# Four softmax attentions of a two-block transformer kernel, regrouped to 512 score columns a step, and differential weights combined ahead of normalising

## The reference, cut to what matters

```
global (8 query heads, 2 key heads, d = 64): softmax(q k^T / 8) v                       512 x 512 scores a head
dilated (3 groups of 4 heads): s = q k^T / 8 + bias, masked to |offset| <= reach
    lse = logsumexp(s); o = exp(s - lse) v
    out = sum over groups of softmax(lse)_group * o_group
differential (8 heads, two score maps m = 0, 1 each, causal):
    p_m = softmax(q_m k_m^T / 8 + rel_bias);  out = (p_0 - lambda p_1) v
window (8 heads, 2 key heads, a query block sees its own and the block before):
    s = q k^T / 8 + bias;  p = exp(s - max) / (sum exp(s - max) + exp(sink - max));  out = p v
```

## Time and profile before

| | |
|---|---|
| median of 3 executions | 3630.17 (3629.97 to 3633.74) |
| profiled execution, its own time | 3633.27 |
| its span | 3631.5 |
| mean granted PE clock over the span | 0.919 of full speed |
| busy: PE, PEld, DVE, ACT, POOL | 3201.4, 2543.0, 2324.2, 1214.5, 374.9 |
| first-layer attention stage, twice | 213.6 to 347.3 and 1097.5 to 1231.2 |
| differential attention stage | 1985.6 to 2087.4 |
| window attention stage | 3131.2 to 3201.2 |

### The profile page before, as it was taken

The page is one execution under the profiler, slowest core; times in us unless marked ns, Lnnn a source line. Parts: engine busy times, 40 slices in busy tenths (PEclk is TensorE's granted clock), DMA queues, the critical chain, the costliest instruction groups (busy, mean ns, idle before and its releaser), DMA issues. The chain is left out here.

```text
span 3631.5 us, 40689 instructions
## 1 busy us (share of the span) xinstructions
PE 3201.4 (88%) x14731; PEld 2543.0 (70%) x14731; DVE 2324.2 (64%) x3761; ACT 1214.5 (33%) x1713; POOL 374.9 (10%) x136
## 2 busy tenths in 40 slices
PE   4999996996799896899499789889999898989999
PEld 3777775774676685777377578757887687658887
DVE  6766666897676657599733747667664575564445
ACT  2323224664323322476322624431111222231111
POOL 0000001000000000100000000304444000004443
PEclk9999996998799998799789799989999899869999
DMA  7751724997655353599652034024442452103222
GB/s 256 238 171 61 242 101 141 360 405 278 216 171 168 135 185 99 193 401 403 243 170 100 1 102 139 27 82 133 148 144 74 136 182 79 53 24 105 92 92 81
DMA packets 285304, 583.89 MB, mean 161 GB/s; under 512 B 21561, under 2 KB 129537, under 8 KB 278076
## 3 DMA queue, kind: packets, MB, share of 16 engines
q1 hardware_dynamic: 272744, 537.83, 42.8%
q10 hardware_dynamic: 7764, 26.85, 1.8%
q0 software_dynamic: 4608, 16.78, 1.2%
HBM read 529.44 MB, written 78.70 MB: 167 GB/s over the span
## 5 line engine op out<-in xcount | busy, mean ns | idle before, releaser
L132 ACT CAST w_hi<-ring 128x2048 fp32r<-128x2048 f32 (+2 forms) x166 | 308.1, 1859 | 1213.5 <-PE ps L283 1030.9
L283 PE MATMUL ps<-hT_hi,w_hi 128*128 128x512 f32 (+1 forms) x1256 | 501.1, 399 | 25.2 <-DVEq L1117 12.6
L283 PE MATMUL ps<-hT_lo,w_hi 128*128 128x512 f32 (+1 forms) x1256 | 498.6, 397 | 0.0
L139 POOL TENSOR_TENSOR w_lo<-ring,w_hi 128x2048 fp32r<-128x2048 f32 x64 | 307.2, 4802 | 935.9 <-ACTq L2854 552.7
L144 DVE TENSOR_TENSOR w_lo<-ring,w_hi 128x2048 fp32r<-128x2048 f32 (+3 forms) x112 | 245.4, 2195 | 233.5 <-ACT w_hi L132 233.2
L283 PE MATMUL ps<-hT_hi,w_lo 128*128 128x512 f32 (+1 forms) x1256 | 305.2, 395 | 10.2 <-DVE w_lo L144 10.2
L283 PEld LDWEIGHTS ps<-hT_hi,w_hi 128*128 128x128 f32 (+1 forms) x1256 | 238.6, 190 | 85.6 <-DVEq L1117 14.2
L283 PEld LDWEIGHTS ps<-hT_hi,w_lo 128*128 128x128 f32 (+1 forms) x1256 | 235.7, 188 | 67.3 <-DVE w_lo L144 12.2
L1054 DVE SCALAR_TENSOR_TENSOR piece_sums<-pieces,cond,piece_sums 128x512 f32<-128x512 f32 x294 | 220.7, 751 | 90.4 <-DMA pieces<-in_w_ada_dram 57.8
L283 PEld LDWEIGHTS ps<-hT_lo,w_hi 128*128 128x128 f32 (+1 forms) x1256 | 238.6, 190 | 55.5
L283 PE MATMUL ps<-w_hi,hT_hi 128*128 128x512 f32 (+1 forms) x672 | 259.9, 389 | 1.0 <-ACT w_hi L132 1.0
(11 more groups left out here) (594 smaller groups left out, 6258.3 us busy)
## 6 DMA issues: line engine op xcount, KB each, us to landing
ring<-in_mlp_w_dram SPq DMA_DIRECT2D x64, 1024.0 KB, 5.2
pieces<-in_w_ada_dram SPq DMA_DIRECT2D x96, 512.0 KB, 6.0
ring<-in_w_in_dram SPq DMA_DIRECT2D x36, 1024.0 KB, 7.0
pieces<-in_mod_w_dram SPq DMA_DIRECT2D x72, 512.0 KB, 5.3
raw_sep<-in_w_exp_gate_dram SPq DMA_DIRECT2D x50, 512.0 KB
raw_sep<-in_w_exp_up_dram SPq DMA_DIRECT2D x50, 512.0 KB
raw_sep<-in_w_exp_down_dram SPq DMA_DIRECT2D x24, 1024.0 KB
ring<-in_e_w_in_dram SPq DMA_DIRECT2D x24, 1024.0 KB, 5.5
```

What stands on the lines that cost most here:

```text
L132: self.k.nc.scalar.copy(self.k.parts[0][:, i, 0:words], self.k.ring[:, i, 0:words]).then_inc(self.high, 1)
L139: self.k.nc.gpsimd.tensor_tensor(self.k.parts[1][:, i, 0:words], self.k.ring[:, i, 0:words], self.k.parts[0][:, i, 0:words].bitcast(F32), ...
L283: mm = pe.matmul(out, a if weight_left else b, b if weight_left else a, start=first and part == 0 and q == ks[0] and o == 0, stop=last and ...
```

## The change

- **Groups.** The units become groups of 512 score columns in one bank: one head of the global attention, four heads of 128 columns, or two heads of 256. First layer: 32 global groups and 16 dilated ones (for each tile two with four heads, two with two). Window: 2 groups of four heads (t = 0) and 12 of two. A group's heads have one parity.
- **Scores.** PE issues the scores of groups a and a+1 together, in every second step; a's heads read partitions 0 to 63, a+1's 64 to 127, and they take turns. The order of the global units changes to suit.
- **Maxima.** DVE takes the maximum of group i+1 in step i (before, of i). With a bias it is now an add and a reduce over all heads. For four dilated heads a third instruction adds the negated maxima by broadcast, and ACT's exponential is one instruction over 512 columns; otherwise one per head. The dilated sums are no longer accumulated: v has a column of ones, so that the product yields 65 columns a head. The signs of maxima and sink are turned, which saves the negation.
- **Copies of transposes** go to ACT for odd global groups and for all dilated and window groups. Scores' and exponentials' buffers become three each.
- **Window.** 28 instead of 12 warm-up matmuls.
- **Differential.** The maxima come out negated (scale -1, minimum) and aren't linked; map 1 is scaled by the ratio of the sums times -lambda and added to unscaled map 0, and ACT's output copy multiplies by map 0's reciprocal. The full-width scaling and the negation are gone.
- **Around it.** `U1` and `U2` become `U12`, heads are stored by parity, `v0`, `v0c`, `vc` get the column of ones, and `branches` merges with the new layout.

The diff, cut to its core:

```diff
 def attention(k, groups, loads=(), space=None, late=(), ahead=None, warm=12):
-        pr, sc, pT = idle[:, 0:4], idle[:, 4:6], idle[:, 6:8]
+        pr, sc, pT = idle[:, 0:3], idle[:, 3:6], idle[:, 6:8]
+        by_act = [u["kind"] != "global" or i % 2 == 1 for i, u in enumerate(groups)]
...
         def _(pe):
+            def scores(a):
+                b = a + 1
+                if b >= 4:
+                    pe.wait_ge(exp_done, b - 3)
+                for h in range(heads(a)):
+                    last_a, last_b = score(a, h), score(b, h)
+                last_a.then_inc(s_ready, 1)
+                last_b.then_inc(s_ready, 1)
+            warm_up(k, pe, 4, warm)
             for i in range(-2, N + 2):
-                if i + 2 < N:
-                    n, u = i + 2, units[i + 2]
-                    if n >= 4:
-                        pe.wait_ge(exp_done, n - 3)
-                    pe.matmul(k.ps[:, bank[n % 4], 0:W(n)], u["q"], u["k"], start=True, stop=True).then_inc(s_ready, 1)
+                if i % 2 == 0 and i + 2 < N:
+                    scores(i + 2)
...
         def _(act):
+            def soften(i):
+                u = groups[i]
+                act.wait_ge(max_done, i + 1)
+                if i >= 3:
+                    act.wait_ge(t_ready, i - 2)
+                if i >= 4 and u["kind"] != "dilated":
+                    act.wait_ge(o_out, i - 3)
+                p = pr[:, i % 3]
+                if u["kind"] == "global":
+                    last = nc.scalar.activation(p, k.ps[:, bank[i % 4], :], ACT.Exp, bias=nm(i), accum_out=ls[:, i % 4, 0:1])
+                elif u["kind"] == "dilated" and heads(i) == 4:
+                    last = nc.scalar.activation(p, sc[:, i % 3], ACT.Exp)
+                else:
+                    if u["kind"] == "window":
+                        nc.scalar.activation(es[:, i % 4, 0:heads(i)], es[:, i % 4, 0:heads(i)], ACT.Exp)
+                    for h in range(heads(i)):
+                        last = nc.scalar.activation(p[:, at], sc[:, i % 3, at], ACT.Exp, bias=nm(i)[:, h:h + 1], accum_out=total)
+                last.then_inc(exp_done, 1)
+            for i in range(N + 1):
+                if i < N:
+                    soften(i)
+                v = i - 1
+                if v >= 0 and by_act[v]:
+                    act.wait_ge(t_ready, v + 1)
+                    if v >= 2:
+                        act.wait_ge(o_ready, v - 1)
+                    nc.scalar.copy(pT[:, v % 2], k.ps[:, 2 + v % 2, :]).then_inc(t_act, 1)
...
         def _(dve):
+            def maxima(i):
...
+                x = per_head(sc[:, i % 3], i)
+                link(V.tensor_tensor(x, per_head(s, i), u["bias"], ALU.add))
+                ins = V.tensor_reduce(nm(i), x, AX, ALU.max, negate=True)
+                if u["kind"] == "window":
+                    link(ins)
+                    link(V.tensor_tensor(nm(i), nm(i), u["less_sink"], ALU.min))
+                    ins = V.tensor_tensor(es[:, i % 4, 0:heads(i)], nm(i), u["less_sink"], ALU.subtract)
+                elif heads(i) == 4:
+                    link(ins)
+                    ins = V.tensor_tensor(x, x, bcast(nm(i), 2, width(i)), ALU.add)
+                ins.then_inc(max_done, 1)
...
+            for i in range(-1, N + 2):
+                if i + 1 < N:
+                    maxima(i + 1)
+                v = i - 1
+                if 0 <= v < N and not by_act[v]:
...
+                    V.tensor_copy(pT[:, v % 2], k.ps[:, 2 + v % 2, :]).then_inc(t_dve, 1)
                 if i >= 2:
+                    result(i - 2)
...
 def diff_attention(...)
-                        pe.wait_ge(max_done, n - 1)
+                        pe.wait_ge(max_done, 2 * n - 2)
-                    nc.scalar.copy(y[:, t, h * P:(h + 1) * P], k.ps[:, 6 + u % 2, 0:P]).then_inc(o_out, 1)
+                    nc.scalar.activation(y[:, t, h * P:(h + 1) * P], k.ps[:, 6 + u % 2, 0:P], ACT.Copy, scale=inv[:, u % 4, 0:1]).then_inc(o_out, 1)
-                        link(V.tensor_tensor_reduce(sc[:, i % 2, m, 0:W(i)], k.ps[:, 2 * (i % 2) + m, 0:W(i)], b, 1.0, 2 * NEG,
-                                                    ALU.add, ALU.max, mx[:, i % 2, m:m + 1]))
-                    V.tensor_scalar(nm[:, i % 2, :], mx[:, i % 2, :], -1.0, None, ALU.mult).then_inc(max_done, 1)
+                        V.tensor_tensor_reduce(sc[:, i % 2, m, 0:W(i)], k.ps[:, 2 * (i % 2) + m, 0:W(i)], b, -1.0, -2 * NEG,
+                                               ALU.add, ALU.min, nm[:, i % 2, m:m + 1]).then_inc(max_done, 1)
...
-                    link(V.reciprocal(l, l))
-                    link(V.tensor_tensor(l[:, 1:2], l[:, 1:2], nlam[:], ALU.mult))
+                    link(V.reciprocal(inv[:, u % 4, :], l))
+                    link(V.scalar_tensor_tensor(r, l[:, 0:1], inv[:, u % 4, 1:2], nlam[:], ALU.mult, ALU.mult))
-                    link(V.tensor_scalar(p0, p0, l[:, 0:1], None, ALU.mult))
-                    V.scalar_tensor_tensor(p0, p1, l[:, 1:2], p0, ALU.mult, ALU.add).then_inc(p_ready, 1)
+                    V.scalar_tensor_tensor(p0, p1, r, p0, ALU.mult, ALU.add).then_inc(p_ready, 1)
```

More of the change, by code:

```diff
@@ L188, in constants @@
         for h in range(BG):
[L189 removed]
+            band[:, e, h % 2, h // 2] = np.where(ok, -slope[h] * dist.astype(f), f(NEG))
     out["bias_band"] = band
@@ L1561, in qkd_dst, with attention @@
     return dst, p, mul
-def attention(k, units, loads=(), space=None, late=(), ahead=None):
+def attention(k, groups, loads=(), space=None, late=(), ahead=None, warm=12):
     nc = k.nc
@@ L1647, in _ @@
             link = Link(dve, step)
[L1648 to L1664, removed]
-                        link(nc.vector.tensor_tensor_reduce(sc[:, i % 2, 0:W(i)], s, u["bias"], 1.0, 2 * NEG, ALU.add, ALU.max, m))
-                        if u.get("sink") is not None:
-                            link(nc.vector.tensor_tensor(m, m, u["sink"], ALU.max))
-                        nc.vector.tensor_scalar(n, m, -1.0, None, ALU.mult).then_inc(max_done, 1)
-                i = ahead - 1
-                if 1 <= i <= N:
-                    v = i - 1
@@ new lines, in result @@
+            def result(v):
+                u, n = groups[v], heads(v)
+                dve.wait_ge(o_ready, v + 1)
+                d = u["heads"][0][2][0].shape[-1]
+                po = k.ps[:, 4 + v % 2, 0:n * d]
+                if u["kind"] == "dilated":
+                    V.tensor_copy(u["out"], po.rearrange("p (h d) -> p h d", h=n)).then_inc(o_out, 1)
+                    return
+                l = ls[:, v % 4, 0:n]
+                if u["kind"] == "window":
+                    link(V.tensor_tensor(l, l, es[:, v % 4, 0:n], ALU.add))
+                link(V.reciprocal(l, l))
+                if n == 1:
+                    V.tensor_scalar(u["out"], po, l, None, ALU.mult).then_inc(o_out, 1)
+                else:
+                    V.tensor_tensor(u["out"], po.rearrange("p (h d) -> p h d", h=n), bcast(l, 2, d), ALU.mult).then_inc(o_out, 1)
@@ new lines, in global_groups, with dilated_groups @@
+    return groups
+def dilated_groups(T, band, cls):
+    groups = []
+    for t in range(NT):
+        for odd in range(2):
+            rows, heads = slice(64 * odd, 64 * odd + 64), []
+            for g in range(2):
+                for half in range(2):
+                    q, kk = (T[n][rows, 2 * g + half, t * P:(t + 1) * P] for n in ("qcT", "kcT"))
+                    heads.append((q, kk, [T["vc"][:, t, BG * g + 2 * half + odd, :]]))
+            u = T["U12"][:, 2 * t + odd].rearrange("p g h d -> p (g h) d")
+            groups.append(dict(kind="dilated", heads=heads, bias=cls[:, odd], out=u[:, :, 0:HD + 1], nm=u[:, :, HD + 1]))
+        for odd in range(2):
+            rows, heads = slice(64 * odd, 64 * odd + 64), []
+            for half in range(2):
+                heads.append((T["q0T"][rows, half, t * P:(t + 1) * P], T["k0T"][rows, half, t * P:t * P + 256],
+                              [T["v0"][:, t + j, 2 * half + odd, :] for j in range(2)]))
+            u = T["U0"][:, 2 * t + odd]
+            groups.append(dict(kind="dilated", heads=heads, bias=band[:, 0 if t == 0 else 2 if t == NT - 1 else 1, odd],
+                               out=u[:, :, 0:HD + 1], nm=u[:, :, HD + 1]))
+    return groups
@@ L3579, in odd_mixer @@
             ring = lambda i: k.ring[:, i, :].rearrange("p (k n) -> p k n", k=4)
-            attention(k, units, space=space, late=moves, ahead=[(ring(i), wo[:, KD:KD + 4, 512 * i:512 * (i + 1)]) for i in range(2)])
+            attention(k, groups, warm=28, space=space, late=moves, ahead=[(ring(i), wo[:, KD:KD + 4, 512 * i:512 * (i + 1)]) for i in range(2)])
             hT = pair_of(nc, h, "hT", [P, KD, S], side="right")
```

207 lines of the change are left out of this document (105 added, 102 removed).

## The result

The changed kernel takes 3523.57 us in the median (3518.82 to 3526.11, 4 runs) against 3630.42 (3629.97 to 3633.74, 4 runs): ratio 0.9702, 95% interval 0.9685 to 0.9719. The profiled execution has a span of 3524.3 us.

What follows compares the result with a forecast made beforehand. PE was taken to bound the global part, DVE and PE nearly tied in the dilated part, in-order PE and low clock mattering elsewhere. Gains of 62 (first layer), 8 (differential) and 7 (window) sum to 77 us: 3553 us, range 3526 to 3582.

Steps and rivals of the forecast that it cites:

- Some fours will stay up: I take 8: Differential stage: gain of 8 us (5 to 20), with the clock up for some sets of four units.
- I take low: 7: Window stage: clock lost in the idle start and low after, gain of 7 us (3 to 22).
- the clock stays up in both: Rival for the differential and window stages: gains of 16 and 21 us, 99 in all, kernel 3531 us; chance 0.20.
- once low, never regained it: Window stage: the old stage never regained the clock level though PE was busy throughout; basis for taking 7 us, not 21.
- a DVE wait for scores of over 1 us in each four: Differential stage: sign expected in the profile, with the stage at about 93 us.
- clock up throughout: Differential stage: four units take 8.9 us against 10.85, a gain of 15.6 us.
- the 2.5 of the rival: Rival for the dilated groups: DVE bounds them at 2.5 us each, gain 64 us, kernel 3566 us; chance 0.16.
- Early maxima and ACT's copies: Global part of the first layer: both moves worth nothing by themselves, hidden in PE's time.
- Loads: First dilated maximum: all loads must have landed, now needed earlier; over 4 us of cover, so cost nothing.
- pairs that don't overlap: Rival for the paired scores: no overlap, global period still 2.48 us, gain 44 us, kernel 3586 us; chance 0.07.
- a low clock in the first layer: Rival: PE falls to the low level there, 3.65 us a group, kernel 78 us slower at 3708; chance 0.04.
- no change: Rival for the whole kernel: time within 0.2% (7 us), gains offset by unseen waits such as late loads; chance 0.02.

Runs made afterwards that it cites:

- late_maxima: The changed kernel with each maximum taken in step i as before, not one group early: 3598.83 us, ratio 0.9892 to the kernel before.
- window_unpaired: The changed kernel with window groups for t > 0 ordered so that both groups of a pair have one parity: 3531.52 us, ratio 0.9727 to the kernel before.
- diff_filled: The kernel before with dummy matmuls where PE idles in the differential stage: 3620.56 us, ratio 0.9971 to the kernel before.
- fused: The changed kernel with each head's add and maximum fused into one DVE instruction: 3507.06 us, ratio 0.9650 to the kernel before.
- copies_dve: The changed kernel with the transposes' copies of all global groups on DVE, none on ACT: 3548.40 us, ratio 0.9744 to the kernel before.
- diff_alone: The kernel before with the change's differential edit and nothing else: 3615.98 us, ratio 0.9950 to the kernel before.

## Why the prediction was wrong

**The step that failed is the clock in the two short stages.** "Some fours will stay up: I take 8" and "I take low: 7" chose the lower end of each range from the behaviour of the old stages. The rival in which the clock stays up in both (62 + 16 + 21 = 99 us, chance 0.20) came nearest: the stages gave 101.9. That is partly luck, for the clock did not stay up in either (0.94 and 0.76).

- Window: the sizes were right (3.55 for 3.65, 2.31 for 2.45, warm-up 3.7 for 3.4), and so was the loss of the level in the idle start. (The forecast's terms for DVE sum to 2.30 to 2.59 and not to the 2.42 to 2.55 that stand there; it changes nothing.) Wrong was "once low, never regained it", read from one trace and carried over. The Trainium skill ("TensorE: Matmul & The Clock Gate", Part 1, What's actually happening) says that activity releases the throttle; the prediction set it aside because the old trace disagreed, and here the level came back behind 12 us of unbroken PE work. So from its first score the stage ran low for 22 of 44.7 us, where the sum had it low throughout. In late_maxima, where PE went on idling about a third or more of every second window of 4 us, it came back for 3.4 us only. Why the old stage did not regain it in 40 us with PE busy throughout stays open: the level can come back without pairing (window_unpaired), and the size of the groups was not tried alone.
- Differential: both terms were undersized. The prediction took 5.6 us for the edit with the clock mixed as before, since DVE's saving would turn into waiting for PE at the low level, and 2.4 more for the clock. The edit is worth 10.5 us at clock 1.00, and the clock the other 8.6 of the stage's 19.1, of the 10.0 that holding it brought the old stage. The forecast sign, a DVE wait for scores of over 1 us in each four, came (0.85 + 0.32 us); the stage's time did not. The prediction's "clock up throughout" (8.9 us for four units, 15.6 in all) was itself 0.3 us a four too high: they take 8.59. At clock 1.00 the old four takes 10.08 us (diff_filled, with its dummies), not 10.85.
- First layer: right within 3 us, partly by cancelling. The global part gave 32 x 0.595 = 19.0 a call for 16.8: overlap 13.6, and 5.4 from taking groups two by two, which was not in the sum. The dilated part took 2.05 for 2.1 and gave 16.5; the ends cost 2.1 for 1.4 in the first call. The second gave 31.9, for 3.4 us at its start ran at the low level. The tie of DVE and PE went to DVE, at 2.05, not at the 2.5 of the rival. The Trainium skill's warning that evacuation may become the bound ("TensorEngine Tiling (Array Packing)", Performance Considerations, PSUM Bottleneck) is borne out in part: in the dilated and window groups DVE, which adds the bias to the scores out of PSUM but also reduces them, was the bound, as fused shows (2.05 to 1.895 us a group); in the global ones it was not.
- Early maxima and ACT's copies were called worth nothing by themselves. Taken out of the change they cost 81 us (both calls and the window stage) and 21 us (both calls) of stage time, what the clock adds included. The sum compared each engine's total with PE's; it should have followed the chain through the banks, and asked what each gap does to the clock.
- Loads: no wait, as forecast. The rivals with pairs that don't overlap, with a low clock in the first layer, and with no change were wrong for the change as made; the low clock in the first layer, given 0.04, is what copies_dve and late_maxima ran into.

## What to carry to other kernels

Where matmuls wait for other engines, price the clock before the work: give each stage a time at either level, hold the level with dummy matmuls in the idle time as an experiment, and take it as gained only where a profile shows it. An engine whose work sums to less than the bound's can still set the pace through a buffer that it frees late; follow the chain for one period. And parts that look free in a sum may be what keeps the others' gain: undo them singly. In a stage whose clock moves between its levels one profile does not price a change.

## What the runs showed of the hardware

A wait of 1.49 us in a stretch in which PE had been nearly always busy was followed by some 27 us at clock 0.50 (copies_dve; 14 us in its second call). A stage of the same code ran at 0.85 in one kernel (diff_alone) and at 0.92 to 0.94 in eight others. The low level ended behind 12 us of unbroken PE work in the changed window stage and did not end in 40 us of it in the old one. Useless matmuls in idle time made a kernel faster (3620.56 against 3633.87 us). Score matmuls on partitions 0 to 63 and 64 to 127 of two 512-column groups took 1.13 us side by side, and 1.98 on the same partitions.
